# Sums of weights on VectorE in two instructions instead of one, each behind the low part that frees its unit

## The chip, the cores and the metric

The kernel runs on one core of one Trainium2 chip. The metric is the device time of one launch in microseconds (us). The kernel before took 3440.4 us, the median of three runs (3439.98 to 3441.76).

## The reference

The program computes three transformer blocks on 256 tokens of width 2048, in float32. Each block has a mixer and a gated feed-forward network. The part that the change touches is the feed-forward network of the first block:

```python
def swiglu(x, w_gu, w_d):
    gate, up = jnp.split(x @ w_gu, 2, axis=-1)
    return (jax.nn.silu(gate) * up) @ w_d
# FFN_HIDDEN = 5632, D_MODEL = 2048
x = layer_norm(DEEPNORM_ALPHA * x + swiglu(x, ffn_wgu[l], ffn_wd[l]), ln2_g[l], ln2_b[l])
```

## The kernel before, in words

**Units and their path.** All big products are made from weights that stream from memory in *units*: 128 partitions by 1024 float32 values, which are two row blocks of 128 rows by 512 columns, 512 KB. A unit goes through four hands. SyncE's queue (SP) loads it into a raw slot (`slot_load`, L248 to L256). ScalarE (ACT) casts it to its high part (`high_part`, L282). VectorE (DVE) subtracts the high part from the raw values and so makes the low part (`low_part`, L301). TensorE (PE) multiplies high by high, low by high and high by low (L341 to L343 in plain blocks, L3647 to L3649 in the items below). Four semaphores tie them: one per raw slot for the landing, `hi_ready`, `lo_ready`, `w_used`. The split slots are a ring: four in most of the kernel, five in the stretch of this change, so ScalarE may cast a unit only when TensorE has used the unit five places before it. A raw slot is loaded anew when the low part of its last user is done. Every engine has the same order of units written out in its own program.

**The stretch with sums.** In the feed-forward network of the first block, hidden columns are taken in chunks of 512 for gate and up. For the first 8 of the 16 row blocks of the weight matrix, the products of two halves of the tokens, two halves of these row blocks and the two column sets (gate and up) are combined in the manner of Strassen: seven products (P1 to P7) take the place of eight, and some of their operands are sums of weight blocks. The other 8 row blocks (gate 4 to 7, up 4 to 7) are multiplied plainly. The weights for this stand in four *quads* of two units each (q = 0 and 1): a, b (raw slots 4 to 7, `quad_ab` and `quad_b`), c and d (slots 8 to 11). Sums are made in place by `weight_sum`: for P5, a + b into a; for P7, b + d into b; for P6, a + d into a; for P4, a + c into a. P1, P2 and P3 use a, c and d as they came. Since the quad a is P1, then P5, P6 and P4 in turn, a sum may be written only when the low part of the product before it has been made, and ScalarE's cast of the next product waits for the sum (`ready("summed")`, L2071).

**The order of a step.** One step has 30 items, a unit each: gate 4, P2, P2, gate 5, P5, P5, gate 6, P6, P6, gate 7, P7, P7, up 4, P4, P4, up 5, P3, P3, up 6, up 7 (`ITEMS`), and then the second product with `ffn_wd`: down 0 to 3, P1, P1, down 4 to 7 (`DOWN`). P1 and the sums for P5 and P7 there belong to the next chunk. There are eight steps: one, a loop of six trips, and a last one with no P1, P5 or P7 sums; ahead of them stands one `DOWN` part alone, which makes the first P1 and the first sums for P5 and P7. That is 8 places for each of the four sums, 32 sums in all. VectorE's order is written out in `sums_step` (L3034) and, for the part ahead, in `down` (L3112): between the low parts stand additions of finished blocks to x (`add_at`, L3039; in the first part L2240), the low parts of turned hidden values (L418), and the gathering of gate and up (L3045 to L3062). In the kernel before, the sum for P6 stands behind the second low part of P5, the sum for P4 behind the second of P6, the sum for P5 one item behind the second of P1, and the sum for P7 two items behind it.

Of the kernel before, what the change touches and what calls it, by code (L numbers as in the profile page):

```python
# [22 lines left out]
ALU = mybir.AluOpType  # L23
# [46 lines left out]
ITEM = {item: i for i, item in enumerate(ITEMS + DOWN)}  # L70
# [98 lines left out]
def build(nc, A, out, upto=99):  # L169
# [732 lines left out]
    def half(n):  # L902
# [65 lines left out]
    side_whole = {name: big(o, [P, 4, P]) for name, o in (("P5", 7168), ("P7", 7680), ("P6", 9216), ("P3", 9728))}  # L968
    up_parts = big(17952, [P, TT, BLK])
    sums_per = {"unit": STEP, "block": 6, "turn": 2, "split_turn": 2, "ring": 16, "split": STEP, "gated": 2,  # L970
                "gate_whole": 1, "summed": 4, "dve_step": 3, "snapped": 4}
    sums_per |= {f"raw{i}": 4 if i < 4 else 1 for i in range(12)}
    SUMS_TRIPS = 6
    sums_from = {}
# [527 lines left out]
    def _(act):  # L1502
        c = Count()
# [506 lines left out]
        def hidden(which):  # L2010
# [53 lines left out]
            def sums_item(item):  # L2064

                what, q = item
                if what in PART:
                    x = PART[what]
                    slot = QUAD[x] + q
                    if what in SUMS:  # L2070
                        act.wait_ge(ready("summed"), c.now("summed", SUMS.index(what) + 1))  # L2071
                    else:
                        act.wait_ge(landed[slot], c.now(f"raw{slot}", 1, 1, 16))
                        c.n[f"raw{slot}"] += 1
                    if what == "P7":
                        c.n[f"raw{slot}"] += 1
                    high_part(act, c, raw_at[slot], UNIT)
                else:
                    unit_hi(act, c, UNIT)

            def sums_step(last=False):

                start, base = c.n["block"], c.n["unit"]

                def snap(to, bank_, unit):
                    act.wait_ge(w_used, c.until(unit))
                    nc.scalar.copy(to, bank(bank_)).then_inc(ready("snapped"), 1)
                    c.n["snapped"] += 1

                def turn_taken(k):  # L2090
                    turn_take_hi(act, c, hT_hi[:, k:k + 2, :].rearrange("p k t -> p (k t)"))

                def gated(m):
                    if m == 0:
                        act.wait_ge(ready("gate_whole"), c.now("gate_whole", 1))
                        c.n["gate_whole"] += 1
                    else:
                        act.wait_ge(acc_free[start % 2], c.freed(start))
                    A_(r[:, m, :], r[:, m, :], ACT.Silu).then_inc(ready("gated"), 1)
                    c.n["gated"] += 1  # L2100

                items = ITEMS + (DOWN_LAST if last else DOWN)
                for i, item in enumerate(items):
                    if i == len(ITEMS):
                        c.n["summed"] += len(SUMS)
                        if last:
                            c.rings(range(RAW_SLOTS))
                    sums_item(item)
                    if i == 0:
                        act.wait_ge(acc_free[(start - 5) % 2], c.freed(start - 5))  # L2110
                        snap(r[:, 0, :], 6, base - 4)
                    if i == ITEM["gate", 4] + 5:
                        turn_taken(0)
                    if i == ITEM["gate", 5] + 5:
                        turn_taken(2)
                    if i == ITEM["P5", 1] + 5:
                        snap(up_parts[:, 1, :], 7, base + ITEM["P5", 1] + 1)
                    if i == ITEM["P6", 1] + 4:
                        snap(up_parts[:, 0, :], 6, base + ITEM["P6", 1] + 1)
                    if i == ITEM["P7", 1] + 5:  # L2120
                        snap(r[:, 1, :], 6, base + ITEM["P7", 1] + 1)
                    if i == ITEM["gate", 7] + 7:
                        gated(0)
                    if i == ITEM["P4", 1] + 7:
                        gated(1)
                c.end = c.n["unit"]
                c.n["block"] += 6
# [99 lines left out]
    def _(dve):  # L2227
# [749 lines left out]
        def hidden(which):  # L2977
# [31 lines left out]
                else:  # L3009
                    unit_lo(dve, c, UNIT)  # L3010

            def landing(x):
                for q in range(2):
                    slot = QUAD[x] + q
                    dve.wait_ge(landed[slot], c.now(f"raw{slot}", 1, 1, 16))
                    c.n[f"raw{slot}"] += 1

            def weight_sum(what):
                if what == "P5":
                    dve.wait_ge(lo_ready, c.now("unit", -1))  # L3020
                    landing("b")
                    ins = TENS(quad_ab, quad_ab, quad_b, ALU.add)
                elif what == "P7":
                    dve.wait_ge(ready("summed"), c.now("summed"))
                    landing("d")
                    ins = TENS(quad_b, quad_b, quad_d, ALU.add)
                else:
                    dve.wait_ge(lo_ready, c.now("unit"))
                    ins = TENS(quad_ab, quad_ab, quad_d if what == "P6" else quad_c, ALU.add)
                ins.then_inc(ready("summed"), 1)  # L3030
                c.n["summed"] += 1

            def sums_step(before, last=False):
# [36 lines left out]
                for i, item in enumerate(items):  # L3070
                    if i == len(ITEMS) and last:
                        c.rings(range(RAW_SLOTS))
                    sums_item(item)
                    if item in (("P5", 1), ("P6", 1)):
                        weight_sum("P6" if item[0] == "P5" else "P4")
                    if not last and i == ITEM["P1", 1] + 1:
                        weight_sum("P5")
                    if i == 2 and before is None:
                        add_at(base - 2, start - 2, 2)
                    if i == 4:  # L3080
                        if before is None:
                            add_at(base, start - 1, 3)
                        else:
                            before()
                    if i == ITEM["gate", 4] + 6:
                        turn_taken(0)
                    if i == ITEM["gate", 5] + 6:
                        turn_taken(2)
                    if i == ITEM["gate", 7] + 5:
                        gate_whole(0)  # L3090
                    if i == ITEM["P4", 1] + 5:
                        gate_whole(1)
                    if i == ITEM["up", 7] + 4:
                        up_whole()
                    if i == ITEM["up", 7] + 5:
                        hidden_whole()
                    if i == ITEM["down", 1] + 5:
                        add_at(base + ITEM["down", 1] + 1, start + 2, 0)
                    if not last and i == ITEM["P1", 1] + 2:
                        weight_sum("P7")  # L3100
                    if not last and i == ITEM["down", 3] + 5:
                        add_at(base + ITEM["down", 3] + 1, start + 3, 1)
                if last:
# [7 lines left out]
            def sums_low(after):  # L3111

                def down(out_):
                    c.rings(range(4), range(SPLIT_SLOTS + 1))
                    for slot in range(12):
                        c.n[f"raw{slot}"] = sums_from["raw"][slot]
                    base, b = c.n["unit"], c.n["block"]
                    for i, item in enumerate(DOWN):
                        sums_item(item)
                        if i == 1:  # L3120
                            out_()
                        if i == DOWN.index(("down", 1)) + 3:
                            first_out(base + DOWN.index(("down", 1)) + 1, b, 0)()
                        if i == DOWN.index(("P1", 1)) + 1:
                            weight_sum("P5")
                        if i == DOWN.index(("P1", 1)) + 2:
                            weight_sum("P7")
                    first_out(base + DOWN.index(("down", 3)) + 1, b + 1, 1)()
                    first_out(base + DOWN.index(("down", 5)) + 1, b + 2, 2)()
                    c.end = c.n["unit"]  # L3130
                    c.n["block"] += 4
                    return add_out(c.end, b + 3, dst, 3)

                after = step(1, after, True, at_down=down)
                sums_step(after)
                with c.loop(dve, SUMS_TRIPS, sums_per):
                    sums_step(None)
                sums_step(None, True)
                c.rings(None, range(SPLIT_SLOTS))
# [739 lines left out]
```

## Time and profile before

| what | value |
|---|---|
| median of the three runs | 3440.4 us |
| the profiled execution's own time | 3441.97 us |
| its span | 3440.0 us |
| PE busy | 3413.3 us (99%) |
| DVE busy | 2093.5 us (61%) |
| ACT busy | 1675.0 us (49%) |
| mean granted TensorE clock | 0.998 |

The span is the time from the first to the last instruction of the profiled execution; 1.97 us of that execution's time lie outside it. A line of the page's fifth part is a group of like instructions with its busy time, the mean of one in ns, and the idle time of its engine ahead of it. Successive matmuls overlap, so a matmul shows 0.39 us although the next one starts 0.23 us after it. VectorE's instructions overlap too at their ends, by about 0.08 us. A row of the timeline has the start, the duration, the engine, the line and the operation, and in brackets the idle time ahead of it. A row of the busy times by stretches has the stretch, its length, then the busy time (and count) of PE, of PE's weight loads, of DVE, ACT and POOL, the granted clock as a share of full speed, the DMA share and GB/s. A row of waits has the total, the number of times and the longest.

### The profile page before, as it was taken

The page shows a single profiled execution, that of the slowest core. Times are in us where ns is not written, and L with a number is a line of the kernel's source. Part 1 is how long each engine was busy: PE and PEld are TensorE (multiplying, and loading weights), DVE is VectorE, ACT ScalarE, POOL GpSimd, SP SyncE. Part 2 cuts the span into 40 slices and gives each one's busy share as a digit, 9 for nine tenths or more (in the row PEclk, how much of TensorE's full clock was granted, in tenths as well). Part 3 has the DMA queues.
Part 4 walks back from the last instruction along what each step waited for, and adds up shares of the span by engine and source line. Part 5 has one row for each costly group of instructions (what it writes and reads, how often), then busy time and mean ns, then how long its engine had stood idle before and what let it go on. Part 6 is the DMA issues. An engine that isn't in the chain of part 4 may idle for free.

```text
span 3440.0 us, 42681 instructions
## 1 busy us (share of the span) xinstructions
PE 3413.3 (99%) x15748; PEld 2795.0 (81%) x15748; DVE 2093.5 (61%) x2299; ACT 1675.0 (49%) x2135; POOL 323.0 (9%) x430
## 2 busy tenths in 40 slices
PE   9999999999999999999999999999999999999999
PEld 8788877888887888777888878888888788888887
DVE  4544586888886755667556545567544845455546
ACT  5444434555554455554444434446556644444443
POOL 0000010000001000002343303000380000000000
PEclk9999999999999999999999999999999999999999
DMA  7555545565565455456555547655554555555554
GB/s 245 169 167 181 201 162 179 194 220 177 199 214 197 156 174 159 133 191 172 188 187 195 188 158 222 203 195 163 192 173 152 166 188 184 194 189 184 188 188 142
DMA packets 333322, 630.19 MB, mean 183 GB/s; under 512 B 33180, under 2 KB 36096, under 8 KB 331648
## 3 DMA queue, kind: packets, MB, share of 16 engines
q1 hardware_dynamic: 326272, 603.20, 53.8%
q0 software_dynamic: 6768, 25.05, 2.3%
q8 instruction: 90, 1.47, 0.2%
q14 instruction: 48, 0.39, 0.0%
q10 hardware_dynamic: 144, 0.07, 0.0%
HBM read 624.86 MB, written 2.33 MB: 182 GB/s over the span
## 4 chain that ended last, share of the span: by engine, by line
PE 96%; DVE 2%; ACT 1%; issue 0%; DMA 0%; SPq 0%; DVEq 0%; ACTq 0%
PE psum L341 25%; PE psum L343 25%; PE psum L342 25%; PE psum L3649 3%; PE psum L3648 3%; PE psum L3647 3%; PE psum L401 3%; PE psum L681 1%; PE psum L1029 1%; PE psum L683 1%; PE psum L682 1%; DVE weights_lo L301 1%; PE psum L1042 0%; PE psum L3545 0%; PE psum L598 0%; PE psum L596 0%
## 5 line engine op out<-in xcount | busy, mean ns | idle before, releaser
L301 DVE TENSOR_TENSOR weights_lo<-weights_raw,weights_hi 128x1024 fp32r<-128x1024 f32 (+1 forms) x1106 | 1369.7, 1248 | 1085.2 <-ACT weights_hi L282 1081.9
L282 ACT CAST weights_hi<-weights_raw 128x1024 fp32r<-128x1024 f32 (+1 forms) x1106 | 1157.4, 1049 | 1513.0 <-PE psum L343 1403.2
L341 PE MATMUL psum<-weights_hi,act_hi 128*128 128x512 f32 x2536 | 1011.7, 399 | 5.2 <-DVE weights_lo L301 5.1
L343 PE MATMUL psum<-weights_hi,act_lo 128*128 128x512 f32 x2536 | 991.1, 391 | 0.0
L342 PE MATMUL psum<-weights_lo,act_hi 128*128 128x512 f32 x2536 | 989.3, 390 | 0.0
L341 PEld LDWEIGHTS psum<-weights_hi,act_hi 128*128 128x128 f32 x2536 | 477.3, 188 | 107.2 <-issue 14.4
L343 PEld LDWEIGHTS psum<-weights_hi,act_lo 128*128 128x128 f32 x2536 | 476.5, 188 | 102.1
L342 PEld LDWEIGHTS psum<-weights_lo,act_hi 128*128 128x128 f32 x2536 | 477.8, 188 | 92.9
L341 PE MATMUL psum<-weights_hi,hid_hi 128*128 128x512 f32 x1284 | 505.4, 394 | 6.1 <-DVE big L3062 3.6
L342 PE MATMUL psum<-weights_lo,hid_hi 128*128 128x512 f32 x1284 | 501.8, 391 | 0.0
L343 PE MATMUL psum<-weights_hi,hid_lo 128*128 128x512 f32 x1284 | 501.7, 391 | 0.0
L341 PEld LDWEIGHTS psum<-weights_hi,hid_hi 128*128 128x128 f32 x1284 | 241.9, 188 | 59.2 <-issue 5.6
L343 PEld LDWEIGHTS psum<-weights_hi,hid_lo 128*128 128x128 f32 x1284 | 242.0, 188 | 51.0
L342 PEld LDWEIGHTS psum<-weights_lo,hid_hi 128*128 128x128 f32 x1284 | 242.0, 188 | 49.2
L401 PE MATMUL psum<-ident,big 128*128 128x128 f32 (+1 forms) x754 | 117.3, 272 | 0.2 <-DVE hid_lo L418 0.2
L401 PEld LDWEIGHTS psum<-ident,big 128*128 128x128 f32 (+1 forms) x754 | 93.4, 139 | 28.8 <-issue 3.4
L2239 DVE TENSOR_TENSOR x<-x,psum 128x1024 f32<-128x1024 f32 x54 | 65.8, 1219 | 60.4 <-PE psum L343 60.4
L3647 PE MATMUL psum<-weights_hi,act_hi 128*128 128x512 f32 x240 | 94.2, 393 | 0.0
L3649 PE MATMUL psum<-weights_hi,act_lo 128*128 128x512 f32 x240 | 93.6, 390 | 0.0
L3648 PE MATMUL psum<-weights_lo,act_hi 128*128 128x512 f32 x240 | 93.6, 390 | 0.0
L994 POOL DMA_DIRECT2D big<-in_ffn_wgu x8 | 5.7, 729 | 813.6 <-DVE big L2747 443.1
L301 DVE TENSOR_TENSOR big<-weights_raw,big 128x1024 fp32r<-128x1024 f32 x49 | 59.9, 1222 | 22.7 <-ACT big L282 22.7
(507 smaller groups left out, 3018.4 us busy)
## 6 DMA issues: line engine op xcount, KB each, us to landing
weights_raw<-in_ffn_wgu SPq DMA_DIRECT2D x312, 512.0 KB, 3.9
weights_raw<-in_w_ff SPq DMA_DIRECT2D x252, 512.0 KB, 3.9
weights_raw<-in_ffn_wd SPq DMA_DIRECT2D x176, 512.0 KB, 4.3
weights_raw<-in_even_w_in SPq DMA_DIRECT2D x120, 512.0 KB, 3.5
weights_raw<-in_w_in SPq DMA_DIRECT2D x64, 512.0 KB, 3.4
weights_raw<-in_odd_w_in SPq DMA_DIRECT2D x60, 512.0 KB, 3.7
big<-in_ffn_wgu SPq DMA_DIRECT2D x32, 512.0 KB, 8.0
weights_raw<-in_odd_w_o SPq DMA_DIRECT2D x32, 512.0 KB, 3.5
```

The source lines that it names most:

```text
L282: nc.scalar.copy(hi_at[to][:, done:size], of[:, done:size]).then_inc(hi_ready, 1)
L301: nc.vector.tensor_tensor(lo_at[to][:, done:size], of[:, done:size], hi_at[to][:, done:size].bitcast(F32), ALU.subtract).then_inc(lo_ready, 1)
L341: nc.tensor.matmul(o, ah, wh, start=(k + j == 0), stop=False)
L342: nc.tensor.matmul(o, ah, wl, start=False, stop=False)
L343: last = nc.tensor.matmul(o, al, wh, start=False, stop=(k + j == kts - 1))
L401: last = nc.tensor.transpose(psum[:w, 4 + t % 2, at_col:at_col + p], src, ident[:p, :p])
L681: nc.tensor.matmul(o, ah, wh, start=(u + j == 0), stop=False)
L682: nc.tensor.matmul(o, ah, wl, start=False, stop=False)
L2239: return TENS(o, o, s, ALU.add)
L3647: nc.tensor.matmul(bank(b), ah, wh, start=start_, stop=False, skip_group_check=True)
L3648: nc.tensor.matmul(bank(b), ah, wl, start=False, stop=False, skip_group_check=True)
L3649: last = nc.tensor.matmul(bank(b), al, wh, start=False, stop=stop, skip_group_check=True)
```

## The change

Each of the four sums is made by two instructions of 128x1024 instead of one of 128x2048, one for each unit q of the quad. The half for q stands right behind the low part that frees the unit q: for P6 behind P5 (q), for P4 behind P6 (q), for P5 behind P1 (q). The halves for P7 stand one and two items behind the second P1. The semaphore `summed` counts eight a step instead of four, and ScalarE's cast of a P item waits for its own half (P7's halves are the third and fourth). Each half of P5 or P7 waits for the landing of its own unit of b or d alone. SyncE's and TensorE's programs stay as they were.

```diff
-                        act.wait_ge(ready("summed"), c.now("summed", SUMS.index(what) + 1))
+                        act.wait_ge(ready("summed"), c.now("summed", 2 * SUMS.index(what) + 1 + q))
...
-            def weight_sum(what):
+            def weight_sum(what, q):
                 if what == "P5":
-                    dve.wait_ge(lo_ready, c.now("unit", -1))
-                    landing("b")
-                    ins = TENS(quad_ab, quad_ab, quad_b, ALU.add)
+                    dve.wait_ge(lo_ready, c.now("unit"))
+                    landing("b", q)
+                    ins = TENS(quad_ab[:, q, :], quad_ab[:, q, :], quad_b[:, q, :], ALU.add)
                 elif what == "P7":
-                    dve.wait_ge(ready("summed"), c.now("summed"))
-                    landing("d")
-                    ins = TENS(quad_b, quad_b, quad_d, ALU.add)
+                    dve.wait_ge(ready("summed"), c.now("summed", -q))
+                    landing("d", q)
+                    ins = TENS(quad_b[:, q, :], quad_b[:, q, :], quad_d[:, q, :], ALU.add)
                 else:
                     dve.wait_ge(lo_ready, c.now("unit"))
-                    ins = TENS(quad_ab, quad_ab, quad_d if what == "P6" else quad_c, ALU.add)
+                    other = quad_d if what == "P6" else quad_c
+                    ins = TENS(quad_ab[:, q, :], quad_ab[:, q, :], other[:, q, :], ALU.add)
...
-                    if item in (("P5", 1), ("P6", 1)):
-                        weight_sum("P6" if item[0] == "P5" else "P4")
-                    if not last and i == ITEM["P1", 1] + 1:
-                        weight_sum("P5")
+                    if item[0] in ("P5", "P6"):
+                        weight_sum("P6" if item[0] == "P5" else "P4", item[1])
+                    if not last and item[0] == "P1":
+                        weight_sum("P5", item[1])
+                    if not last and i - 1 == ITEM["P1", 1]:
+                        weight_sum("P7", 0)
...
                     if not last and i == ITEM["P1", 1] + 2:
-                        weight_sum("P7")
+                        weight_sum("P7", 1)
```

VectorE's order in the `DOWN` part ahead of the first step, from the low part of P1's first unit (written to `big_62`) to that of down 7, before. L3022 is the sum for P5, L3026 the sum for P7, L2240 the addition of a finished block to x:

```order
L301 TENSOR_TENSOR big_62<-weights_raw,big_61 128x1024 [waits hi_ready]
L2240 SCALAR_TENSOR_TENSOR x<-x,psum 128x2x512 [waits w_used]
L301 TENSOR_TENSOR weights_lo<-weights_raw,weights_hi 128x1024 [waits hi_ready] x2
L3022 TENSOR_TENSOR weights_raw<-weights_raw 128x2048 [waits unit_landed7,unit_landed6,lo_ready]
L301 TENSOR_TENSOR weights_lo<-weights_raw,weights_hi 128x1024 [waits hi_ready]
L3026 TENSOR_TENSOR weights_raw<-weights_raw,big_60 128x2048 [waits unit_landed11,unit_landed10,end_then_summed]
L301 TENSOR_TENSOR weights_lo<-weights_raw,weights_hi 128x1024 [waits hi_ready]
L301 TENSOR_TENSOR big_62<-weights_raw,big_61 128x1024 [waits hi_ready]
```

The same place in the changed kernel, where L3021 is half a sum for P5 and L3025 half a sum for P7:

```order
L301 TENSOR_TENSOR big_62<-weights_raw,big_61 128x1024 [waits hi_ready]
L2240 SCALAR_TENSOR_TENSOR x<-x,psum 128x2x512 [waits w_used]
L3021 TENSOR_TENSOR weights_raw<-weights_raw 128x1024 [waits unit_landed6,lo_ready]
L301 TENSOR_TENSOR weights_lo<-weights_raw,weights_hi 128x1024 [waits hi_ready]
L3021 TENSOR_TENSOR weights_raw<-weights_raw 128x1024 [waits unit_landed7,lo_ready]
L301 TENSOR_TENSOR weights_lo<-weights_raw,weights_hi 128x1024 [waits hi_ready]
L3025 TENSOR_TENSOR weights_raw<-weights_raw,big_60 128x1024 [waits unit_landed10,end_then_summed]
L301 TENSOR_TENSOR weights_lo<-weights_raw,weights_hi 128x1024 [waits hi_ready]
L3025 TENSOR_TENSOR weights_raw<-weights_raw,big_60 128x1024 [waits unit_landed11,end_then_summed]
L301 TENSOR_TENSOR weights_lo<-weights_raw,weights_hi 128x1024 [waits hi_ready]
L301 TENSOR_TENSOR big_62<-weights_raw,big_61 128x1024 [waits hi_ready]
```

Two halves of P5 now stand ahead of the low part of down 4, where before no sum stood, and the second half of P7 moved behind the low part of down 5.

VectorE's order in a step between P5 and gate 7, before. L3029 is the sum for P6 (with `big_60`) and for P4 (with `big_59`), L418 the low part of turned hidden values, and the last row but one the low part of gate 7:

```order
L2239 TENSOR_TENSOR x<-x,psum 128x2x512 [waits w_used]
L301 TENSOR_TENSOR weights_lo<-weights_raw,weights_hi 128x1024 [waits hi_ready]
L3029 TENSOR_TENSOR weights_raw<-weights_raw,big_60 128x2048 [waits lo_ready]
L301 TENSOR_TENSOR weights_lo<-weights_raw,weights_hi 128x1024 [waits hi_ready]
L418 TENSOR_TENSOR hid_lo<-psum,hid_hi 128x512 [waits turn_hi]
L301 TENSOR_TENSOR weights_lo<-weights_raw,weights_hi 128x1024 [waits hi_ready] x2
L3029 TENSOR_TENSOR weights_raw<-weights_raw,big_59 128x2048 [waits lo_ready]
L301 TENSOR_TENSOR big_62<-weights_raw,big_61 128x1024 [waits hi_ready]
L418 TENSOR_TENSOR hid_lo<-psum,hid_hi 128x512 [waits turn_hi]
```

The same place in the changed kernel, from the low part of P5's first unit to that of gate 7:

```order
L301 TENSOR_TENSOR big_62<-weights_raw,big_61 128x1024 [waits hi_ready]
L3029 TENSOR_TENSOR weights_raw<-weights_raw,big_60 128x1024 [waits lo_ready]
L2239 TENSOR_TENSOR x<-x,psum 128x2x512 [waits w_used]
L301 TENSOR_TENSOR weights_lo<-weights_raw,weights_hi 128x1024 [waits hi_ready]
L3029 TENSOR_TENSOR weights_raw<-weights_raw,big_60 128x1024 [waits lo_ready]
L301 TENSOR_TENSOR weights_lo<-weights_raw,weights_hi 128x1024 [waits hi_ready]
L418 TENSOR_TENSOR hid_lo<-psum,hid_hi 128x512 [waits turn_hi]
L301 TENSOR_TENSOR weights_lo<-weights_raw,weights_hi 128x1024 [waits hi_ready]
L3029 TENSOR_TENSOR weights_raw<-weights_raw,big_59 128x1024 [waits lo_ready]
L301 TENSOR_TENSOR weights_lo<-weights_raw,weights_hi 128x1024 [waits hi_ready]
L3029 TENSOR_TENSOR weights_raw<-weights_raw,big_59 128x1024 [waits lo_ready]
L301 TENSOR_TENSOR big_62<-weights_raw,big_61 128x1024 [waits hi_ready]
```

One half of each sum moved ahead by one low part; all four halves still stand ahead of the low part of gate 7.

## Rows read from the trace of the kernel before

**Rows 1.** The page: busy time and share of each engine, with instruction counts.
```profile
PE 3413.3 (99%) x15748; PEld 2795.0 (81%) x15748; DVE 2093.5 (61%) x2299; ACT 1675.0 (49%) x2135; POOL 323.0 (9%) x430
```
**Rows 2.** Busy time by stretches; the sums run from about 575 to 1082.
```profile
575.00:1082.00 507.00, 507.00 (x2256) 417.55 (x2255) 428.01 (x370) 280.47 (x301) 8.87 (x14) 1.00 0.58 196
```
**Rows 3.** Who waited for whom, 560 to 1100 (two rows), then 575 to 1082 (one).
```profile
PE psum L341 <- DVE big L3062: 3.6, 1, 3.6
PE psum L341 <- DVE weights_lo L301: 2.5, 1, 2.5
...
ACT weights_hi L282 <- DVE weights_raw L3029: 14.7, 8, 1.9
```
**Rows 4.** VectorE's timeline in the part ahead, behind P1's first low part.
```profile
572.87 1.22 DVE L2240 SCALAR_TENSOR_TENSOR x<-x,psum 128x1024 f32<-128x1024 f32 x1
574.00 2.36 DVE L301 TENSOR_TENSOR weights_lo<-weights_raw,weights_hi 128x1024 fp32r<-128x1024 f32 x2
576.27 2.28 DVE L3022 TENSOR_TENSOR weights_raw<-weights_raw 128x2048 f32<-128x2048 f32 x1
578.47 1.22 DVE L301 TENSOR_TENSOR weights_lo<-weights_raw,weights_hi 128x1024 fp32r<-128x1024 f32 x1
...
584.08 1.21 DVE L2240 SCALAR_TENSOR_TENSOR x<-x,psum 128x1024 f32<-128x1024 f32 x1
```
**Rows 5.** TensorE's first weight loads of down 4 and down 6 there.
```profile
580.09 0.19 PEld L341 LDWEIGHTS psum<-weights_hi,hid_hi 128*128 128x128 f32 x1
...
585.58 0.19 PEld L341 LDWEIGHTS psum<-weights_hi,hid_hi 128*128 128x128 f32 x1
```
**Rows 6.** SyncE's queue: the loads of b's second and of d's second unit.
```profile
558.42 0.52 SPq L255 DMA_DIRECT2D weights_raw<-in_ffn_wgu  x1
...
565.25 0.47 SPq L255 DMA_DIRECT2D big<-in_ffn_wgu  x1
```
**Rows 7.** The page: loads into the quads c and d, median time to landing.
```profile
big<-in_ffn_wgu SPq DMA_DIRECT2D x32, 512.0 KB, 8.0
```
**Rows 8.** VectorE's timeline in the first trip, from P5's first low part to gate 7.
```profile
656.48 1.23 DVE L301 TENSOR_TENSOR big<-weights_raw,big 128x1024 fp32r<-128x1024 f32 x1 [1.56 <-ACT big L282]
657.63 1.22 DVE L3039 TENSOR_TENSOR x<-x,psum 128x1024 f32<-128x1024 f32 x1
659.22 1.23 DVE L301 TENSOR_TENSOR weights_lo<-weights_raw,weights_hi 128x1024 fp32r<-128x1024 f32 x1 [0.38 <-ACT weights_hi L282]
660.48 2.29 DVE L3029 TENSOR_TENSOR weights_raw<-weights_raw,big 128x2048 f32<-128x2048 f32 x1
...
663.83 0.68 DVE L418 TENSOR_TENSOR hid_lo<-psum,hid_hi 128x512 fp32r<-128x512 f32 x1
664.43 2.35 DVE L301 TENSOR_TENSOR weights_lo<-weights_raw,weights_hi 128x1024 fp32r<-128x1024 f32 x2
666.82 2.29 DVE L3029 TENSOR_TENSOR weights_raw<-weights_raw,big 128x2048 f32<-128x2048 f32 x1
669.02 1.22 DVE L301 TENSOR_TENSOR big<-weights_raw,big 128x1024 fp32r<-128x1024 f32 x1
```
**Rows 9.** TensorE's first weight loads of P6's second unit and of gate 7.
```profile
670.90 0.19 PEld L3647 LDWEIGHTS psum<-weights_hi,big 128*128 128x128 f32 x1
...
672.26 0.19 PEld L3647 LDWEIGHTS psum<-big,act_hi 128*128 128x128 f32 x1
```
**Rows 10.** VectorE's timeline around the sum for P5, end of the first step.
```profile
632.68 1.22 DVE L301 TENSOR_TENSOR big<-weights_raw,big 128x1024 fp32r<-128x1024 f32 x1
...
637.35 1.23 DVE L301 TENSOR_TENSOR weights_lo<-weights_raw,weights_hi 128x1024 fp32r<-128x1024 f32 x1 [1.10 <-ACT weights_hi L282]
```
**Rows 11.** TensorE's first weight load of down 4 in that step.
```profile
643.99 0.19 PEld L341 LDWEIGHTS psum<-weights_hi,hid_hi 128*128 128x128 f32 x1
```
**Rows 12.** The chain of waits behind the stretch, where TensorE stands still.
```profile
1085.64 1.30 DVE big L3062 x2
...
1086.98 0.50 PE psum L341
```

More of the change, by code:

```diff
@@ L970, in build @@
     sums_per = {"unit": STEP, "block": 6, "turn": 2, "split_turn": 2, "ring": 16, "split": STEP, "gated": 2,
-                "gate_whole": 1, "summed": 4, "dve_step": 3, "snapped": 4}
+                "gate_whole": 1, "summed": 8, "dve_step": 3, "snapped": 4}
     sums_per |= {f"raw{i}": 4 if i < 4 else 1 for i in range(12)}
@@ L2104, in sums_step @@
                     if i == len(ITEMS):
-                        c.n["summed"] += len(SUMS)
+                        c.n["summed"] += 2 * len(SUMS)
                         if last:
@@ L3010, in sums_item, with landing @@
                     unit_lo(dve, c, UNIT)
[L3012 to L3016, printed above, removed]
-            def weight_sum(what):
+            def landing(x, q):
+                slot = QUAD[x] + q
+                dve.wait_ge(landed[slot], c.now(f"raw{slot}", 1, 1, 16))
+                c.n[f"raw{slot}"] += 1
+            def weight_sum(what, q):
                 if what == "P5":
-                    dve.wait_ge(lo_ready, c.now("unit", -1))
-                    landing("b")
-                    ins = TENS(quad_ab, quad_ab, quad_b, ALU.add)
+                    dve.wait_ge(lo_ready, c.now("unit"))
+                    landing("b", q)
+                    ins = TENS(quad_ab[:, q, :], quad_ab[:, q, :], quad_b[:, q, :], ALU.add)
                 elif what == "P7":
-                    dve.wait_ge(ready("summed"), c.now("summed"))
-                    landing("d")
-                    ins = TENS(quad_b, quad_b, quad_d, ALU.add)
+                    dve.wait_ge(ready("summed"), c.now("summed", -q))
+                    landing("d", q)
+                    ins = TENS(quad_b[:, q, :], quad_b[:, q, :], quad_d[:, q, :], ALU.add)
                 else:
                     dve.wait_ge(lo_ready, c.now("unit"))
-                    ins = TENS(quad_ab, quad_ab, quad_d if what == "P6" else quad_c, ALU.add)
+                    other = quad_d if what == "P6" else quad_c
+                    ins = TENS(quad_ab[:, q, :], quad_ab[:, q, :], other[:, q, :], ALU.add)
                 ins.then_inc(ready("summed"), 1)
@@ L3123, in down @@
                             first_out(base + DOWN.index(("down", 1)) + 1, b, 0)()
[L3124 to L3127, printed above, removed]
+                        if item[0] == "P1":
+                            weight_sum("P5", item[1])
+                        if i in (DOWN.index(("P1", 1)) + 1, DOWN.index(("P1", 1)) + 2):
+                            weight_sum("P7", i - DOWN.index(("P1", 1)) - 1)
                     first_out(base + DOWN.index(("down", 3)) + 1, b + 1, 1)()
```

## The prediction

> **What bounds the kernel now.** I read the page's busy times first: TensorE is busy for 3413.3 of 3440.0 us, VectorE for 61% [rows 1]. So at most 26.7 us of the span are TensorE standing still, and a change on VectorE gains only where VectorE makes it stand still. Next the busy times by stretches: all eight steps with sums lie between 575 and 1082 us, and there TensorE is busy for 507.00 of 507.00 us, at the full clock (1.00), while VectorE is busy for 428.0 and so idle for 79 [rows 2]. Third the waits: from 560 to 1100 TensorE waited twice, 2.5 us for a low part and 3.6 us for L3062 [rows 3]. The 2.5 us lie ahead of 575, before the first sum. The 3.6 us lie behind 1082, at the end of the last step, which has no sum for P5 or P7. There the chain runs over L3062 at 1085.64 [rows 12]; the last sum stands far ahead of it, before gate 7 of that step. The sums make nobody wait but ScalarE, whose cast of P6's first unit stood for the whole sum 8 times, 14.7 us in all [rows 3]; ScalarE has 226 us of idle time in this stretch (507 less 280.5) [rows 2] and TensorE did not feel it.
>
> The question is therefore not what the change frees but whether it breaks TensorE's cover. The cover is the lead of the low parts: how long before TensorE's first weight load of a unit its low part has ended.
>
> **What the change costs VectorE.** Two 1024 pieces for one 2048: a sum of 2048 takes 2.20 us of the queue (576.27 to 578.47 in [rows 4]); 1024 elements take 1.14 (half of 574.00 to 576.27, two low parts). Two make 2.27, so 0.07 more a sum. Second, a half that stands right behind the low part it waits for can't overlap with that one's end: from the low part at 659.22 to the sum behind it are 1.26 us instead of 1.14 [rows 8], so 0.12 to 0.13 a wait; I take 0.13. Before, P6 and P4 had that wait (2 a step) and P5 and P7 did not. After, both halves of P5, P6 and P4 have it (6), P7's don't, since a low part lies between. Per step 4 x 0.07 + 4 x 0.13 = 0.80 us, and over 8 steps 6.4 us more of VectorE's time, against 79 idle. It costs TensorE nothing unless the lead is gone at one place, so I replay the three tight places from the rows.
>
> *The tightest, gate 7.* Before, its low part starts at 669.02 and ends at 670.24, TensorE loads at 672.26: lead 2.0 us [rows 8, 9]. I take an x addition at 1.13 and L418 at 0.60, as its row and the next. After: P5's first low part 656.48, P6's first half 657.74, x addition 658.88, P5's second low part 660.01 (its cast was done before 659.22), P6's second half 661.27, gate 6 at 662.41 (662.70 before), L418 663.54, P6's first low part 664.14 (its cast no longer waits for the whole sum), P4's first half 665.40, P6's second low part 666.54, P4's second half 667.80, gate 7 at 668.94. That is 0.08 earlier than before, with a lead of 2.1: the added 0.40 us (two splits, two waits) fits into the 0.46 us from 658.76 to 659.22 in which VectorE stood waiting. If that gap couldn't be used, gate 7 would be 0.4 later and the lead 1.6. P6's second unit is what gets later: its low part from 665.56 (the second of the pair at 664.43) to 666.54. It ends at 667.76, loaded at 670.90 [rows 9]: lead 3.1 instead of 4.1.
>
> *P5 and P7 in a step.* P1's first low part 632.68 [rows 10], P5's first half 633.94, the two L3062 from 635.08 (1.20 together: 1.30 in [rows 12] less the overlap), P1's second low part 636.28, P5's second half 637.54, down 4's low part 638.68 instead of 637.35. It ends at 639.9, TensorE loads at 643.99 [rows 11]: lead 4.1 instead of 5.4. L3062 moves back by 1.2 us; what it frees is asked for only in the next step. The raw slot of gate 4 is freed 1.3 us later, at 639.9, and its load starts that much later. Its unit stands four behind down 4, and a unit of 12 matmuls at 0.23 takes 2.7 us, so TensorE wants it near 655.
>
> *The part ahead of the steps* has the least room. From L2240 at 572.87 [rows 4]: P5's first half 574.00, low part 575.14, P5's second half 576.40, down 4's low part 577.54, P7's first half 578.68, low part 579.81, P7's second half 580.95, low parts 582.09 and 583.22, L2240 at 584.35 instead of 584.08. Down 4's low part ends at 578.76, loaded at 580.09: lead 1.3 instead of 3.7 [rows 5]. And L2240 frees the accumulator for down 6: it ends at 585.56 instead of 585.29, and TensorE wants it at 585.58 [rows 5]. From the end of an instruction of VectorE to TensorE's start some 0.04 us pass (L3062 ended at 1086.94, and TensorE, which waited for it, went on at 1086.98 [rows 12]). So this wait may last 0.02 to 0.04 us, once. Its bounds: 0 if a half is a little cheaper, 0.3 if every added piece is twice what I take.
>
> *Landings.* The halves come earlier than the sums did, P5's by up to 2.3 us in the part ahead (574.00 against 576.27), and each waits for its unit of b or d. The sum before ran at 576.27 with both units of b landed, so a half can be held until then at the latest: 2.3 us of TensorE, once, as the upper bound; in a step by the same reckoning to 638.49 (637.35 and 1.14 [rows 10]), 0.5 us more than the lead of 4.1, seven times. I take 0: b's second unit was issued at 558.42, 15.6 us ahead of P5's first half, d's second at 565.25, 15.7 us ahead of P7's second half [rows 6], and such a load lands after some 8 us [rows 7].
>
> **A rule against the rows.** The successive starts here are 1.14 us apart though each low part lasts 1.22 [rows 4], and the wait adds 0.12. The Trainium skill, "VectorE: DVE Perf Modes", section "The DRAIN you can't avoid", says that the next operation does not start until the pipe is empty and that a semaphore costs nothing extra. The trace disagrees with both. By that rule the four added waits of a step would cost nothing and a split 2.44 less 2.28 us, 0.16; the two splits ahead of gate 7 then cost 0.32 instead of 0.40, and the time is again 3440.5.
>
> **The sum.** TensorE: 0.0 us in the steps, 0.0 to 0.1 in the part ahead, 0.0 behind. Against the profiled execution (span 3440.0 and 1.97 around it, 3441.97) that stays 3442.0; the median of the runs is 1.6 lower, so I forecast 3440.5.
>
> **Rivals.**
> 1. *VectorE's cover breaks at gate 7, slower.* Four halves and their waits stand ahead of that low part. If they cost more than 2.0 us over the whole sums, TensorE stops in every step. I took 0.4 for them; it needs five times that, 0.5 us a half. At 1.0 us more a half it is 4.0 less 2.0, so 2.0 a step, 8 steps 16 us: 3456. For it: all added work falls where the lead is shortest. Against: the sums are the same kind of instruction with the same operands as the low parts of 1024, whose cost the rows show at 1.22, and the wait's price stands there too [rows 8]. 3%.
> 2. *A stall ends that I hold for foreign, faster.* If the earlier casts of P6 and P4 ran on to the 3.6 us wait for L3062 [rows 3], it would go: 3436.9. But between the last half sum and this place VectorE and ScalarE wait for TensorE and for loads, so the earlier cast is lost. The Trainium skill, "Perfetto Trace Analysis", section "Optimizing Scalar/DVE Operations", says that where these engines are not saturated but cause bubbles on others, breaking up instructions may finish work sooner. The first half of its condition holds here, the second doesn't: the bubbles caused by sums are on ScalarE alone. 1%, and even the 3.6 us are 0.1%.
> 3. *The split doesn't do what it says*, and ScalarE still waits as before. Then the time is the same too, 3440.5, and only ScalarE's row would tell. I count it under the forecast, a tenth of it.
> 4. *TensorE's spacing itself moves*, through other traffic in the memory it reads. A matmul every 0.23 us makes the 507; a change of 1% would be 5 us either way, 3435 or 3446. Against: TensorE is busy without a gap in a stretch where VectorE alternates between work and rest. 2%, both signs.
>
> **Chances and range.** The forecast has 94%, the rivals 3, 1 and 2. About 0.2% (7 us) is what a measurement of this kernel tells from no change. Within it: 94 and rivals 2 and 4, and some of rival 1 at a small price: 96%. Faster 1%, slower 3%. The unknown terms reach from 0 to 2.3 us (a late landing), with all of it near 0; the three runs alone spread over 1.8 us. Twice that spread to each side of 3440.5 gives 3436.9 to 3444.1.
>
> **What would show it.** In the changed kernel's profile: between 575 and 1082 TensorE busy without a gap and the same 3.6 us wait for L3062 behind; 64 sums of about 1.22 us in place of 32 of 2.29; VectorE's busy time some 5 us up; ScalarE's 14.7 us wait for L3029 gone or under 3 us; the low part of gate 7 within 0.3 us of its old place relative to TensorE's load, and at down 6 of the part ahead a wait of under 0.1 us or none. I am wrong if TensorE shows a wait for L301 within the steps, or if VectorE waits for a landing there.

## The result, and the profile after

The changed kernel took 3446.43 us (median of 20 runs, 3444.39 to 3448.6), the kernel before 3441.22 in the same rounds (20 runs, 3438.61 to 3445.91): 1.0015 times as long, 95% interval 1.0008 to 1.0022. It is slower by about 5 us, which is under 0.2% but clear of noise, and above the range forecast. The profiled execution has a span of 3443.4 us (3440.0 before) and took 3445.39.

Busy time of the changed kernel in the stretch of the steps; columns are PE, PE's weight loads, DVE, ACT, POOL, clock, DMA share, GB/s:

```profile
575.00:1082.00 507.00, 502.84 (x2227) 411.29 (x2226) 429.49 (x399) 278.62 (x300) 8.87 (x14) 1.00 0.57 192
```

TensorE, which stood still for nothing there [rows 2], now does for 4.2 us by the records. Who made it wait between 560 and 1100 us in the changed kernel (total, times, longest):

```profile
PE psum L341 <- DVE big L3062: 5.7, 8, 2.6
...
PE psum L341 <- DVE weights_lo L301: 2.5, 1, 2.5
...
PE psum L341 <- DVE x L2240: 1.0, 1, 1.0
```

The wait for L3062 has gone from once to 8 times [rows 3]. The wait of ScalarE for L3029 is gone from this view, as it was meant to be. L3062 multiplies gate and up into the hidden values. Behind it the kernel raises the count `acc_free`, and TensorE may write the second product's next block only when that count has come. L3062 reads no accumulator itself. The last reader of the one that this block is written in is L3053, which in the changed kernel was over at 632.25:

```profile
631.57 0.68 DVE L3053 TENSOR_TENSOR big<-psum,big 128x512 f32<-128x512 f32 x1
```

VectorE's timeline in the changed kernel at the end of the first step, which answers to [rows 10]:

```profile
633.37 1.21 DVE L301 TENSOR_TENSOR big<-weights_raw,big 128x1024 fp32r<-128x1024 f32 x1
634.62 1.23 DVE L3021 TENSOR_TENSOR weights_raw<-weights_raw 128x1024 f32<-128x1024 f32 x1
635.76 1.28 DVE L3062 TENSOR_TENSOR big<-big,big 128x512 f32<-128x512 f32 x2
636.96 1.22 DVE L301 TENSOR_TENSOR weights_lo<-weights_raw,weights_hi 128x1024 fp32r<-128x1024 f32 x1
```

And TensorE's first weight load of down 2 in the changed kernel:

```profile
637.10 0.19 PEld L341 LDWEIGHTS psum<-weights_hi,hid_hi 128*128 128x128 f32 x1 [0.90 <-DVE big L3062]
```

The same two places in the kernel before:

```profile
633.82 1.29 DVE L3062 TENSOR_TENSOR big<-big,big 128x512 f32<-128x512 f32 x2
```
```profile
635.79 0.19 PEld L341 LDWEIGHTS psum<-weights_hi,hid_hi 128*128 128x128 f32 x1
```

Before, L3062 ended at 635.11 (633.82 and 1.29) and TensorE wanted the accumulator at 635.79: a lead of 0.68 us. From the low part of P1's first unit to L3062 there were 1.14 us before (632.68 [rows 10] to 633.82) and are 2.39 now (633.37 to 635.76), 1.25 more, for one half sum and its wait. So TensorE should wait 1.25 less 0.68, and 0.04 for the release, 0.61 us. The loss itself is read from the starts of the last matmul of each unit. Those of the unit ahead of down 2 and of down 2, in the kernel before:

```profile
635.78 0.39 PE L343 MATMUL psum<-weights_hi,hid_lo 128*128 128x512 f32 x1
...
638.50 0.39 PE L343 MATMUL psum<-weights_hi,hid_lo 128*128 128x512 f32 x1
```

and in the changed kernel:

```profile
636.24 0.39 PE L343 MATMUL psum<-weights_hi,hid_lo 128*128 128x512 f32 x1
...
639.77 0.39 PE L343 MATMUL psum<-weights_hi,hid_lo 128*128 128x512 f32 x1
```

The unit took 2.72 us and takes 3.53. Compared in this way between the two traces, TensorE falls back at down 2 by 0.67 to 0.69 us in five of the seven steps, by 0.81 in the first and by 1.07 in the fourth, where a load had come later and, through ScalarE's cast, held VectorE: 5.3 us in all.

The idle time in the view of waits reads lower. For the same seven steps, 590 to 1075 us of the changed kernel, it gives

```profile
PE psum L341 <- DVE big L3062: 3.2, 7, 0.8
```

since a matmul shows 0.39 us where the next one comes 0.23 us later: the first 0.16 us of a gap lie under the record ahead of it. The first matmul behind a gap also shows 0.50 us instead of 0.39, 0.11 more:

```profile
637.10 0.50 PE L341 MATMUL psum<-weights_hi,hid_hi 128*128 128x512 f32 x1 [0.48 <-DVE big L3062]
```

Seven times 0.16 and 0.11 are 1.9 us, which with the 3.2 makes most of the 5.3.

In the last step, where L3062 waits for late loads, its wait shrank from 3.6 us [rows 3] to 2.6: TensorE came later, the loads did not come as much later. The stretches around it, of the kernel before and then of the changed one:

```profile
1082.00:1092.00 10.00, 6.44 (x22) 4.83 (x21) 7.48 (x9) 3.45 (x4) 0.00 (x0) 0.83 1.05 386
```
```profile
1087.00:1097.00 10.00, 7.42 (x33) 5.79 (x32) 9.12 (x11) 4.19 (x4) 0.00 (x0) 1.00 1.04 382
```

The granted clock, 0.83 before (part of the stretch at 1.2 instead of 2.4 GHz), stayed at 1.00. The unit of the stall took 7.98 us before and takes 5.64 (from the starts of the last matmuls). That gives back 2.3 of the 5.3 us in this execution.

### The profile page after: what moved, and what is told of

Same layout as the page of the kernel before. It is cut to its first block, busy times and chain, and to the rows that moved or that the text cites. A ratio compares the mean times of both kernels' runs of the same rounds, so it can differ in the third digit from the quotient of the medians.

```text
span 3443.4 us, 42741 instructions
## 1 busy us (share of the span) xinstructions
PE 3413.7 (99%) x15748; PEld 2791.2 (81%) x15748; DVE 2096.6 (61%) x2331; ACT 1674.6 (49%) x2135; POOL 323.0 (9%) x430
## 4 chain that ended last, share of the span: by engine, by line
PE 94%; DVE 3%; DMA 1%; ACT 1%; issue 1%; SPq 0%; DVEq 0%; POOL 0%; ACTq 0%; POOLq 0%
PE psum L341 25%; PE psum L343 25%; PE psum L342 25%; PE psum L401 3%; PE psum L3651 3%; PE psum L3649 3%; PE psum L3650 3%; DMA weights_raw<-in_ffn_wd 1%; PE psum L681 1%; PE psum L1029 1%; PE psum L683 1%; PE psum L682 1%; DVE weights_lo L301 1%; PE psum L1042 0%; DVE big L301 0%
## 5 line engine op out<-in xcount | busy, mean ns | idle before, releaser
L301 DVE TENSOR_TENSOR weights_lo<-weights_raw,weights_hi 128x1024 fp32r<-128x1024 f32 (+1 forms) x1106 | 1370.1, 1248 | 1076.5 <-ACT weights_hi L282 1072.7
L3649 PE MATMUL psum<-weights_hi,act_hi 128*128 128x512 f32 x240 | 94.2, 392 | 0.0
L301 DVE TENSOR_TENSOR big<-weights_raw,big 128x1024 fp32r<-128x1024 f32 x49 | 59.8, 1221 | 22.3 <-ACT big L282 22.3
```

The source lines that it names most:

```text
L301: nc.vector.tensor_tensor(lo_at[to][:, done:size], of[:, done:size], hi_at[to][:, done:size].bitcast(F32), ALU.subtract).then_inc(lo_ready, 1)
L3649: nc.tensor.matmul(bank(b), ah, wh, start=start_, stop=False, skip_group_check=True)
```

## Experiments

Times are medians; "before" is the kernel before in the same rounds.

| kernel | us | before | ratio (95% interval) |
|---|---|---|---|
| L3062 ahead of the half sum | 3441.29 | 3440.52 | 1.0001 (0.9992 to 1.0010) |
| P5 alone split | 3446.51 | 3440.52 | 1.0016 (1.0007 to 1.0025) |
| P6 and P4 alone split | 3440.86 | 3440.52 | 1.0000 (0.9991 to 1.0009) |
| no split, L3062 later | 3452.17 | 3440.52 | 1.0033 (1.0021 to 1.0045) |
| no split, L3053 to L3062 earlier | 3437.40 | 3440.88 | 0.9991 (0.9982 to 1.0000) |
| all split, L3053 to L3062 earlier | 3438.00 | 3440.88 | 0.9992 (0.9983 to 1.0001) |
| no split, these and L2240 earlier | 3437.40 | 3440.88 | 0.9990 (0.9981 to 0.9999) |
| before again, one run | 3441.36 | 3440.88 | |

**1. Undo one place.** The changed kernel with all sums split, but in the steps the half sum for P5 behind L3062:

```diff
-                    if not last and item[0] == "P1":
-                        weight_sum("P5", item[1])
+                    if not last and item == ("P1", 1):
+                        weight_sum("P5", 1)
...
                     if i == ITEM["up", 7] + 5:
                         hidden_whole()
+                        if not last:
+                            weight_sum("P5", 0)
```

> The changed kernel, but in the steps the first half of P5's sum stands behind the two L3062 instead of ahead of them; everything else of the split stays. Theory A (TensorE's down 2 waits for the accumulator that L3062 frees, the lead was 0.63 us, and the half sum in front takes 1.26): the seven waits of 0.6 to 1.1 us are gone, only the wait for L3062 in the last step (3.6 us before) stays; time within 1.3 us of the kernel before. Rival B (VectorE's added time and waits in general, 0.8 us a step): nothing gained, about 5 us above before. Rival C (late loads in the part ahead of the steps): also 5 us above before, with waits for L2240 or for low parts there.

Time as before, and of the waits for L3062 only the last step's is left. In its trace, 560 to 1110 us:

```profile
PE psum L341 <- DVE big L3062: 3.7, 1, 3.7
...
PE psum L341 <- DVE x L2240: 0.9, 1, 0.9
```

VectorE does exactly the same work as in the changed kernel. So the added work (rival B) costs nothing. The wait for L2240 in the part ahead stays, and the time is that of the kernel before all the same: rival C falls too.

**2. One part alone: P5.** The kernel before with only P5's sum split and put as in the changed kernel:

```diff
-                    if not last and i == ITEM["P1", 1] + 1:
-                        weight_sum("P5")
+                    if not last and item[0] == "P1":
+                        weight_sum("P5", item[1])
...
```

The part ahead has the same edit. The counts of `summed` and the splitting of `weight_sum` that go with it are left out here, and in experiment 3.

> The kernel before with only P5's sum split, each half behind its low part as in the changed kernel; P7, P6 and P4 whole and where they were. Theory A: the whole loss comes with this part, 7 waits of about 0.69 us, less what the last step gives back (up to 2.3), plus up to 1.3 in the part ahead: 3 to 6 us above before, as the changed kernel. Rival B: VectorE's added time is 0.33 us of 0.80 a step, so about 2 us above before.

```profile
PE psum L343 <- DVE big L3067: 6.7, 8, 2.5
```

This is the wait for L3062, whose line is L3067 here. The whole loss comes with this part: 6.0 us above before, 0.0016. In six of the seven steps TensorE falls back by 0.65 to 0.75 us, as in the changed kernel. In the first it falls back by 3.4 in this trace, because ScalarE had waited 3.7 us for a load there; so this profile alone doesn't price the place.

**3. The other part: P6 and P4.** The kernel before with only these two split:

```diff
-                    if item in (("P5", 1), ("P6", 1)):
-                        weight_sum("P6" if item[0] == "P5" else "P4")
+                    if item[0] in ("P5", "P6"):
+                        weight_sum("P6" if item[0] == "P5" else "P4", item[1])
```

> The kernel before with only P6's and P4's sums split, each half behind its low part; P5 and P7 whole and where they were. Theory A: no wait of TensorE anywhere in the steps, 0 us (within 0.5) against before. Rival B: 0.40 us of 0.80 a step, so about 2.5 us above before. ScalarE's 14.7 us wait for L3029 gone under either.

```profile
PE psum L343 <- DVE big L3067: 3.3, 1, 3.3
```

No wait in the steps and no time, neither lost nor won. ScalarE's wait for the sums, 14.7 us [rows 3], is gone here and gave TensorE nothing. What it waits for instead is TensorE: the casts of these items stood longer for a free split slot, before (575 to 1082 us) and in this kernel:

```profile
ACT weights_hi L282 <- PE psum L3649: 61.7, 96, 1.7
```
```profile
ACT weights_hi L284 <- PE psum L3654: 77.7, 110, 1.7
```

**4. The place without the split.** The kernel before, nothing added to VectorE, only L3062 one low part later:

```diff
-                    if i == ITEM["up", 7] + 5:
+                    if i == ITEM["up", 7] + 6:
                         hidden_whole()
```

> The kernel before, with no sum split; only the two L3062 stand one low part later in each of the eight steps (behind the second low part of P1, and in the last step one item later too). Theory A: L3062 ends at 637.0 instead of 635.1 in the first step, TensorE's wait is 1.3 us in each of seven steps and 1.2 longer in the last, less what the last gives back: 6 to 10 us above before. Rival B: nothing was added to VectorE, 0 us.

```profile
PE psum L341 <- DVE big L3062: 11.8, 8, 4.6
```

It is 11.6 us slower than before, above the 6 to 10 expected: TensorE falls back by 1.25 us in six steps and 1.8 in the first, as expected, but the last step, where L3062 itself stands behind one more low part, gave nothing back and cost 1.0. A place alone, without one more instruction, so costs twice what the change did.

**5 and 6. More lead.** In all steps L3053 to L3056 one item earlier and L3062 right behind them, once in the kernel before, once in the changed one:

```diff
-                    if i == ITEM["up", 7] + 4:
+                    if i == ITEM["up", 7] + 3:
                         up_whole()
-                    if i == ITEM["up", 7] + 5:
+                    if i == ITEM["up", 7] + 3:
                         hidden_whole()
```

> The kernel before, no sum split; in every step the gathering of gate and up (L3053 to L3056) stands one item earlier and the two L3062 right behind it, ahead of the low parts of down 3 and of P1's first unit. Theory A: L3062's lead before down 2 grows from 0.6 us to about 2 in the steps, which gives nothing there, but in the last step L3062 no longer stands behind a low part whose weights come late: the 3.6 us wait is gone, 3 to 5 us below before. Rival: the last step is bound by the loads themselves, so the wait comes back as one for low parts, 0 us.

> The changed kernel (all four sums split) with the same earlier place of L3053 to L3062. Theory A: the half sum now stands behind L3062, the seven waits are gone, and the last step's too: the same time as the unsplit kernel with this order, within 1 us, so 3 to 5 us below before and 8 to 10 below the changed kernel. Rival B (the split costs VectorE time that tells): 5 us above the unsplit one.

Both are some 3 us below before (3.5 and 2.9, where 3 to 5 were expected), and 0.6 us apart, which the rounds don't tell from nothing. Their intervals just reach 1, so that they are faster at all is likely, not shown, by the medians; their traces show the wait gone. Against the changed kernel's 3446.43, from other rounds, the sixth is 8.4 us faster with the same instructions on VectorE in another order. The busy times of the changed kernel with this order:

```profile
575.00:1082.00 507.00, 507.00 (x2255) 417.16 (x2254) 432.48 (x405) 280.90 (x302) 8.90 (x14) 1.00 0.58 196
1082.00:1092.00 10.00, 9.90 (x44) 7.85 (x43) 7.50 (x7) 3.85 (x4) 0.00 (x0) 1.00 1.05 387
```

TensorE is without a gap again between 575 and 1082 us with all 64 half sums in place, and the stall of the last step is gone as well, with the low clock behind it: its unit takes 2.72 us in experiments 5, 6 and 7 instead of 7.98. A small part comes back two units later, where a unit takes 3.15 to 3.35 us instead of 2.79; the traces of experiments 5 and 7 show a wait for an addition to x there (L3039, 0.2 and 0.3 us). VectorE's timeline there, in the kernel before with this order:

```profile
1077.72 0.69 DVE L3053 TENSOR_TENSOR big<-psum,big 128x512 f32<-128x512 f32 x1
...
1079.53 1.28 DVE L3062 TENSOR_TENSOR big<-big,big 128x512 f32<-128x512 f32 x2
```

L3062 ends at 1080.81 instead of 1086.94 [rows 12]. It had not needed the late loads; it only stood in the queue behind two low parts that did.

**7. The part ahead.** The unsplit kernel of experiment 5 with the second L2240 moved up:

```diff
-                    first_out(base + DOWN.index(("down", 3)) + 1, b + 1, 1)()
+                        if i == len(DOWN) - 2:
+                            first_out(base + DOWN.index(("down", 3)) + 1, b + 1, 1)()
```

> As the first of this call (no split, L3053 to L3062 earlier), and in the part ahead of the steps the second L2240 stands one low part earlier, ahead of that of down 7. Theory A: the wait of 0.8 to 1.0 us for L2240 that the other experiments' traces show is gone; time 0 to 1 us below the first kernel of this call, which these rounds hardly tell.

No wait for L2240 in its trace, but experiment 5's had none either, and the medians are equal: whether it brings anything stays open. Its interval (0.9981 to 0.9999) is the only one below 1; its median is that of experiment 5.

**8. A second profile of the kernel before.**

> The kernel before, unchanged, for a second profile of it. If the 0.8 to 1.3 us wait for L2240 in the part ahead comes from the change, this profile has none, as the first; if it comes from how the loads fall in an execution, it may show it here too.

```profile
PE psum L341 <- DVE big L3062: 2.8, 1, 2.8
PE psum L341 <- DVE x L2240: 0.9, 1, 0.9
```

The unchanged kernel shows the wait for L2240 as well. In this execution the L2240 that frees the accumulator for down 6, the first of the two in the row below, ended 1.2 us behind the moment at which TensorE could have gone on:

```profile
584.42 2.34 DVE L2240 SCALAR_TENSOR_TENSOR x<-x,psum 128x1024 f32<-128x1024 f32 x2
```
```profile
585.69 0.19 PEld L341 LDWEIGHTS psum<-weights_hi,hid_hi 128*128 128x128 f32 x1 [1.30 <-DVE x L2240]
```

So this wait isn't the change's. In the profile on which the prediction rests TensorE came to this place 1.15 us later than here and VectorE's L2240 0.34 us earlier (584.08 [rows 4]), so there it was over in time. The wait for L3062 in the last step, 3.6 us there, is 2.8 here: it too varies by execution. Counted by the length of its unit against 2.72 us, that stall cost 5.3 us in the first profile, 4.5 in this one, 5.3 in experiment 1 and 5.9 in experiment 3.

## Why the prediction was wrong

**What bounds the kernel** was read rightly: the sums made only ScalarE wait, and taking that away gave nothing (experiment 3).

**The step that failed** is one sentence in "P5 and P7 in a step": "L3062 moves back by 1.2 us; what it frees is asked for only in the next step." The 1.2 us were right (1.25 measured). The rest was wrong. L3062 increments `acc_free`, and the down block of units 2 and 3 in the same step waits for it, 0.68 us behind its end. I had treated low parts as the only cover in the steps, with leads of 2.0 us and more, and looked for accumulators only in the part ahead, where I found one at 0.29 us. The smallest lead in a step was not at gate 7, but at an accumulator, and no row of the prediction showed it. The row of down 2's weight load would have: the same view as [rows 11], four units (8.2 us) earlier, at 635.79. And L3062's own row names no accumulator (`big<-big,big`); that it releases one stands in the program alone.

**The replay of the low parts** held. Gate 7's low part was to have a lead of 2.1 us; in the changed kernel it starts as the first row shows, and TensorE loads as the second shows (L3649 there is L3647 of the kernel before):

```profile
670.20 1.22 DVE L301 TENSOR_TENSOR big<-weights_raw,big 128x1024 fp32r<-128x1024 f32 x1
```
```profile
673.52 0.19 PEld L3649 LDWEIGHTS psum<-big,act_hi 128*128 128x128 f32 x1
```

So it ends 2.1 us ahead of TensorE's load. The price of a half, 1.14 us, and of the wait on the low part ahead, 0.12, held too: from the low part at 633.37 to the half sum are 1.25 us, and to the next instruction 1.14. The rule that the prediction sets against its rows would have given the same time, and so missed too. The Trainium skill, "VectorE: DVE Perf Modes", section "The DRAIN you can't avoid", also says that a next operation that isn't held back starts earlier. So the overlap of 0.08 us is no disagreement with it, as the prediction has it; the 0.12 us of a wait is. VectorE's busy time went up by 3.1 us (2093.5 to 2096.6), not by 5.

**The landings** cost nothing, as taken: VectorE itself waited for no load in the steps of the changed kernel. So neither of the two signs came by which the prediction wanted to be found wrong, a wait of TensorE for L301 in the steps or one of VectorE for a landing; the sign that came was the end of TensorE's gapless 507 us.

**The part ahead** was forecast at 0.02 to 0.04 us and showed 1.0 us (by the view of waits). But the kernel before shows 0.9 in its second profile, so what the change adds there is near 0.1 (the unit behind the wait takes 4.03 us in the changed kernel, 3.91 in that profile): VectorE's part of the replay came out (from P1's low part at 572.22 to L2240 at 584.83 are 12.61 us, and 571.74 to 584.35 were forecast, 12.61). What I had taken for fixed were the moments at which the two engines come there: in the changed kernel's profile VectorE's low part of P1 started 0.48 us later than in the first profile, ahead of any half sum of that part, and TensorE was 0.86 earlier.

**Rival 1** had the right kind, a cover that breaks in every step, and the wrong place and price (16 us at gate 7, 3%). **Rival 2**, that the last step's 3.6 us wait could go, did not happen through the split. But I held that wait for the loads' own, and experiments 5 and 6 show that it was an order's. **Rival 3** fell: ScalarE's wait for L3029 is gone. **Rival 4** fell too: apart from the stalls a unit of 12 matmuls takes 2.72 us in both kernels. **The range** fell short because it was built on the spread of runs around a loss of zero; the failed step left 5 us out. Nor was a difference of 0.2% lost in the noise, as the prediction took it: the interval reaches 0.0007 to either side, and 5 us show.

The rule that rival 2 cites from the Trainium skill, "Perfetto Trace Analysis", section "Optimizing Scalar/DVE Operations", says that breaking up instructions may finish work sooner where these engines cause bubbles on others. Here the sums' bubbles were ScalarE's; experiment 3 ended them and gained nothing (1.0000), and the split of P5 made seven new ones on TensorE, by what it was put ahead of.

**What stays open:** the two traces differ by 3.4 us, the medians by 5.2. The interval of the ratio (2.8 to 7.6 us) holds both. The profiled run of the kernel before took 0.8 us more than its median and that of the changed kernel 1.0 less, which is the difference; what varies between the runs wasn't sought. The wait in the last step is one such thing, and how much it gives back on average wasn't measured. No run raises `acc_free` right behind the last reader of the accumulators instead of behind L3062. In the changed kernel's first step L3056, the last of them, ended at 633.45, 3.0 us before TensorE could have begun down 2 (0.23 us behind 636.24). But the same count also tells TensorE that the hidden values are ready to be turned, and ScalarE that it may copy over what L3062 reads (L2110), so these would need a count of their own.

## What to carry to other kernels

Before an instruction is put into an in-order queue, list for everything behind it what it releases, accumulators as well as operands, and for each the lead before its consumer, in the same step; the smallest decides, and it need not be the one that the bottleneck shows as tight. Where a release stands behind work that doesn't touch what is released, its lead is shorter than it need be. A busy bottleneck (507 of 507 us) says that no lead is short by more than a record hides, 0.16 us here, not how far the others reach. And a wait that ends with an instruction which did not need the late thing itself can be had back by order alone, as in experiments 5 and 6.

## What the runs showed that was not expected

- The stall of the last step, 3.6 us by the view of waits, cost the kernel before 5.3 us: its unit took 7.98 us and takes 2.72 with no stall (experiments 5 and 6). The granted clock in that stretch was 0.83, at 1.00 where the wait was 2.6 us (the changed kernel, 5.64 us). What hides in a gap between records and the low clock behind it make the difference. In the second profile of the kernel before the wait was 2.8 us, the clock 0.83 again and the unit took 7.23.
- In the trace of experiment 5 the granted clock falls in one place, some 340 us behind the last step with sums, where it was 1.00 in the kernel before. TensorE loses 1.6 us at one unit there. Experiment 7's trace shows the same (0.91, 1.6 us), experiment 6's and the second one of the kernel before don't (1.00). The cause wasn't sought:

```profile
1420.00:1440.00 20.00, 20.00 (x98) 15.78 (x97) 11.03 (x26) 5.64 (x7) 0.00 (x0) 0.91 0.33 111
```
